# Two transformer blocks on one core: four PSUM banks for the mixers' gate projections, the last one in halves, a head rotation moved, and the retention's value product in three fp32r products

## What is computed

```python
# mixer stage, each of two layers; h is the normalised x, three branches
uv, c_q, c_kv, k_rope, z, xbc, dt_raw, gates = jnp.split(h @ w_in[l], IN_OFFSETS, axis=-1)
y_a = gmlp_mixer(uv, ...)                      # "a": spatial gating
y_b = mla_mixer(c_q, c_kv, k_rope, cos, sin, ...)   # "b": attention, 8 heads
y_c = ssd_mixer(z, xbc, dt_raw, ...)           # "c": scan over two chunks of 128 tokens
g = jax.nn.sigmoid(gates).reshape(bsz, s, N_BRANCH, D_MODEL)
merged = g[:, :, 0] * (y_a @ w_branch[l, 0]) + g[:, :, 1] * (y_b @ w_branch[l, 1]) \
       + g[:, :, 2] * (y_c @ w_branch[l, 2])
x = x + merged @ w_out[l]
# retention, each of four heads: att is the weighted score matrix, vn the values
o = jnp.einsum('bhij,bhjv->bhiv', att, vn) + ...
```

## Time and profile before

| what | value |
|---|---|
| median of 3 runs | 3313.93 us (3313.74 to 3315.62) |
| profiled execution, its own time | 3314.97 us |
| its span, first to last instruction | 3313.2 us |
| mean granted TensorE clock | 0.987 |
| PE busy | 3198.2 us, 97% |
| DVE busy | 1944.1 us, 59% |
| ACT busy | 1294.7 us, 39% |
| chain that ended last | PE 89%, DVE 5%, issue 2%, ACT 2% |

### The profile page before, as it was taken

How to read it: one execution, slowest core, us unless ns; L and a number is a source line. 1 busy time by engine, 2 the same in 40 slices (tenths; PEclk the granted TensorE clock), 3 DMA queues, 4 the chain that set the end, 5 groups by cost and what they waited for, 6 DMA issues and landing times.

```text
span 3313.2 us, 42938 instructions
## 1 busy us (share of the span) xinstructions
PE 3198.2 (97%) x17262; PEld 2727.8 (82%) x17262; DVE 1944.1 (59%) x2685; ACT 1294.7 (39%) x1785; POOL 103.3 (3%) x144
## 2 busy tenths in 40 slices
PE   8999889999998899999999999999999999999898
PEld 8988779899887799788877777778887888887797
DVE  6868568867686577674243344577334753345655
ACT  5446444444464454422223322232223222245543
POOL 1000000000000000000000000000000000022000
PEclk9999999999998999999999999999999999999999
DMA  7754347767553376553323222145333533253354
GB/s 242 243 188 166 112 139 258 248 210 235 177 171 122 127 237 224 174 179 109 114 90 101 77 89 77 64 163 168 99 111 108 188 130 105 99 134 89 98 183 153
DMA packets 334911, 496.96 MB, mean 150 GB/s; under 512 B 11042, under 2 KB 221884, under 8 KB 334716
## 3 DMA queue, kind: packets, MB, share of 16 engines
q1 hardware_dynamic: 330652, 483.46, 43.9%
q0 software_dynamic: 4064, 10.77, 1.5%
HBM read 493.09 MB, written 1.10 MB: 149 GB/s over the span
## 4 chain that ended last, share of the span: by engine, by line
PE 89%; DVE 5%; issue 2%; ACT 2%; POOL 1%; DMA 0%; DVEq 0%; POOLq 0%; ACTq 0%
PE bank L531 28%; PE bank L532 28%; PE bank L533 28%; DVE wlo L1550 1%; PE bank L953 1%; ACT whi L1090 1%; PE bank L661 1%; PE bank L544 1%; PE bank L676 0%; PE bank L938 0%; POOL small L2357 0%; POOL small L2362 0%; DVE bank L2294 0%; DVE small L2290 0%; ACT npr L1498 0%
## 5 line engine op out<-in xcount | busy, mean ns | idle before, releaser
L1550 DVE TENSOR_TENSOR wlo<-raw,whi 128x1024 fp32r<-128x1024 f32 (+1 forms) x780 | 933.9, 1211 | 995.6 <-ACT whi L1090 993.7
L1090 ACT ACTIVATE whi<-raw 128x1024 fp32r<-128x1024 f32 (+1 forms) x780 | 813.5, 1049 | 1189.8 <-PE bank L533 1186.9
L531 PE MATMUL bank<-xTh,whi 128*128 128x256 f32 (+1 forms) x3200 | 1045.5, 327 | 6.1 <-DVE xTl L1606 6.0
L533 PE MATMUL bank<-xTh,wlo 128*128 128x256 f32 (+1 forms) x3200 | 1039.4, 325 | 0.0
L532 PE MATMUL bank<-xTl,whi 128*128 128x256 f32 (+1 forms) x3200 | 1039.3, 325 | 0.0
L531 PEld LDWEIGHTS bank<-xTh,whi 128*128 128x128 f32 x3200 | 610.6, 191 | 68.7 <-issue 19.7
L533 PEld LDWEIGHTS bank<-xTh,wlo 128*128 128x128 f32 x3200 | 610.3, 191 | 49.1
L532 PEld LDWEIGHTS bank<-xTl,whi 128*128 128x128 f32 x3200 | 610.7, 191 | 48.3 <-issue 0.5
L531 PE MATMUL bank<-whi,hh 128*128 128x512 f32 x968 | 377.6, 390 | 0.0
L533 PE MATMUL bank<-whi,hl 128*128 128x512 f32 x968 | 376.7, 389 | 0.0
L532 PE MATMUL bank<-wlo,hh 128*128 128x512 f32 x968 | 376.6, 389 | 0.0
(11 more groups left out here) (337 smaller groups left out, 2318.4 us busy)
## 6 DMA issues: line engine op xcount, KB each, us to landing
raw<-in_ffn_w_in_dram SPq DMA_DIRECT2D x176, 1024.0 KB, 5.4
raw<-in_ffn_w_out_dram SPq DMA_DIRECT2D x80, 1024.0 KB, 5.0
mraw<-in_w_mod_dram SPq DMA_DIRECT2D x72, 1024.0 KB, 5.1
raw<-in_w_in_dram SPq DMA_DIRECT2D x44, 1024.0 KB, 5.1
raw<-in_ret_w_in_dram SPq DMA_DIRECT2D x24, 1024.0 KB, 5.1
raw<-in_w_branch_dram SPq DMA_DIRECT2D x12, 1024.0 KB, 5.0
raw<-in_nat_w_qkv_dram SPq DMA_DIRECT2D x12, 1024.0 KB, 5.1
raw<-in_ffn_w_out_dram SPq DMA_DIRECT2D x16, 512.0 KB, 3.6
```

The costliest lines, as they stand in the source:

```text
L531: pe.matmul(ps, lh, rh, start=start, stop=False, skip_group_check=True)
L533: return pe.matmul(ps, ll, rh, start=False, stop=stop, skip_group_check=True)
L1090: nc.scalar.activation(hi, src, ACT.Copy).then_inc(*e.inc("hi", key, part))
L1550: nc.vector.tensor_tensor(lo, src, hi.bitcast(F32), ALU.subtract).then_inc(*e.inc("lo", key, part))
```

## The change

1. **Rings.** `SHORT` becomes banks 0 to 3 and `LONG` banks 4 to 7. The gates get four banks. `bp`, `ty` of `yb` and `z`, `yd` and `yo` of chunk 1 and `wop` take `SHORT`; `ty` of `merged` takes `LONG`; the sums of chunk 1 take `VALUES` and `TURNED`, which are banks of `LONG`. The neighbourhood attention's rings keep their banks under the new names.
2. **Order of the last gate.** Gate (2,1) is loaded and projected in two halves, the first around the transposes of `yb` and `z`, the second between branch products, which are reordered to (1,0), (2,0), (1,1), (2,1); the last runs whole after the transposes of `merged`.
3. **Steps on ACT and DVE.** A head step's first half stands ahead of the weight splits of that part, its exponentials behind them; DVE asks GpSimd (POOL) for the heads' norms earlier than it reads them; tile 1's rotation moves behind the merges of branch 0.
4. **Retention.** `rv` is kept as `rvh` and `rvl`, `ra` as `rah` and `ral` (7 more DVE subtractions and 3 more ACT copies of 128x512 a head), and `retained` does 36 fp32r matmuls where it did 12 plain ones. `gbm` moves to another place in SBUF, and its two loads on POOL wait for the last head's weights.

```diff
-ALL, SCORES, TURNED, VALUES, UPPER = tuple(range(8)), (0, 1, 2, 3), (4, 5), (6, 7), (4, 5, 6, 7)
+SHORT, LONG = (0, 1, 2, 3), (4, 5, 6, 7)
+ALL, TURNED, VALUES = tuple(range(8)), (4, 5), (6, 7)
...
-        def branch(br):
-            for n in range(2):
-                s.add(("b", l, br, n), rows(w["w_branch"][l, br], 0, 4, 512 * n, 512), 4, 512)
+        def branch(br, n):
+            s.add(("b", l, br, n), rows(w["w_branch"][l, br], 0, 4, 512 * n, 512), 4, 512)
         gate(0, 0)
         gate(0, 1)
-        branch(0)
+        branch(0, 0)
+        branch(0, 1)
         gate(1, 0)
         gate(1, 1)
         gate(2, 0)
-        branch(1)
-        gate(2, 1)
-        branch(2)
+        c = GATES + 2 * D + 512
+        s.add((("g", l, 2, 1), 0), rows(m, 0, 4, c, 512), 4, 512)
+        branch(1, 0)
+        s.add((("g", l, 2, 1), 1), rows(m, 4, 4, c, 512), 4, 512)
+        branch(2, 0)
+        branch(1, 1)
+        branch(2, 1)
...
-        rv = arena("rv", [P, 4, 512], 8 * KB)
+        rvh = arena("rvh", [P, 4, 512], 8 * KB, F32R)
+        rvl = arena("rvl", [P, 4, 512], 74 * KB, F32R)
         rg = arena("rg", [P, 4, 512], 16 * KB)
         ra = arena("ra", [P, 3, 512], 24 * KB)
+        rah = arena("rah", [P, 3, 512], 82 * KB, F32R)
+        ral = arena("ral", [P, 3, 512], 24 * KB, F32R)
...
-        gbm = arena("gbm", [P, 2, D], 74 * KB)
-        rcst = arena("rcst", [P, R_END], 86 * KB)
+        gbm = arena("gbm", [P, 2, D], 30 * KB)
...
-                def gate(br, n, between=lambda part: None):
-                    ps = {t: new("gp", l, br, n, t, ring=LONG if br else ALL) for t in range(2)}
+                def gate_banks(br, n):
+                    return {t: new("gp", l, br, n, t, ring=LONG if br else ALL) for t in range(2)}
+                def gate_part(br, n, ps, part):
+                    rows_by((("g", l, br, n), part // 2), ("gp", l, br, n), ps, *xT[256], 2 * part, 8, (part % 2,))
+                def gate(br, n, step=-6):
+                    ps = gate_banks(br, n)
                     for part in range(4):
-                        rows_by((("g", l, br, n), part // 2), ("gp", l, br, n), ps, *xT[256], 2 * part, 8, (part % 2,))
-                        between(part)
-                def branch(br, n, yT):
-                    token_major([("b", l, br, n)], ("bp", l, br, n), range(2), *yT)
+                        gate_part(br, n, ps, part)
+                        attention(step + part)
+                def branch(br, n, yT, ring=SHORT):
+                    token_major([("b", l, br, n)], ("bp", l, br, n), range(2), *yT, ring=ring)
...
-                        ps = new("csb", l, c, h2)
+                        ps = new("csb", l, c, h2, ring=VALUES if c else ALL)
...
+                    ps = new("csp", l, c, ring=TURNED if c else ALL)
...
+                    ps = new("cbp", l, c, ring=TURNED if c else ALL)
...
-                    ps = new("yd", l, c)
+                    ps = new("yd", l, c, ring=SHORT if c else ALL)
...
-                gate(1, 0, lambda part: (head_turned(0) if part == 1 else attention(part - 2) if part > 1 else None))
+                gate(1, 0, -2)
...
-                ps = new("yo", l)
+                ps = new("yo", l, ring=SHORT)
...
-                gate(1, 1, lambda part: attention(2 + part))
-                gate(2, 0, lambda part: attention(6 + part))
-                turn_y(("b", l), yb, 4, 256, ("yb", l))
-                turn_y(("c", l), z, 4, 256, ("yc", l))
+                gate(1, 1, 2)
+                gate(2, 0, 6)
+                g21 = gate_banks(2, 1)
+                gate_part(2, 1, g21, 0)
+                turn_y(("b", l), yb, 4, 256, ("yb", l), SHORT)
+                gate_part(2, 1, g21, 1)
+                turn_y(("c", l), z, 4, 256, ("yc", l), SHORT)
                 pe.wait_ge(*e.at("yT", ("b", l), 1))
-                for n in range(2):
-                    branch(1, n, ytT[1])
-                gate(2, 1)
+                branch(1, 0, ytT[1])
+                gate_part(2, 1, g21, 2)
+                gate_part(2, 1, g21, 3)
                 pe.wait_ge(*e.at("yT", ("c", l), 3))
                 branch(2, 0, ytT[0])
+                branch(1, 1, ytT[1])
...
+                        ps = new("ty", ("m", l), u, ring=LONG)
...
-                b2 = {t: new("bp", l, 2, 1, t) for t in range(2)}
-                rows_by(("b", l, 2, 1), ("bp", l, 2, 1), b2, *ytT[0], 0, 4, (0,))
                 merged_turned(0)
-                rows_by(("b", l, 2, 1), ("bp", l, 2, 1), b2, *ytT[0], 2, 4, (1,))
+                branch(2, 1, ytT[0])
...
+                    wo[n] = {t: new("wop", l, n, t, ring=SHORT) for t in range(2)}
...
-                pe.wait_ge(*e.at("ra", h, 2))
-                pe.wait_ge(*e.at("rv", h, 3))
+                pe.wait_ge(*e.at("ral", h, 2))
+                pe.wait_ge(*e.at("rvl", h, 3))
                 for t in range(4):
                     ps = new("rop", h, t)
                     if t < 2:
-                        pairs = [(ra[:, 0, 256 * jt + t * P:256 * jt + (t + 1) * P], jt) for jt in range(2)]
-                        pairs += [(ra[:, 1 + jt, t * P:(t + 1) * P], 2 + jt) for jt in range(2)]
+                        pairs = [(0, 256 * jt, jt) for jt in range(2)] + [(1 + jt, 0, 2 + jt) for jt in range(2)]
                     else:
-                        pairs = [(ra[:, 1 + jt, t * P:(t + 1) * P], 2 + jt) for jt in range(2)]
-                    for i, (a, j) in enumerate(pairs):
-                        m = pe.matmul(ps[:, :], a, rv[:, j, :], start=i == 0, stop=i == len(pairs) - 1)
+                        pairs = [(1 + jt, 0, 2 + jt) for jt in range(2)]
+                    for i, (u, c, j) in enumerate(pairs):
+                        cols_of = slice(c + t * P, c + (t + 1) * P)
+                        m = mm3(ps[:, :], rah[:, u, cols_of], ral[:, u, cols_of], rvh[:, j, :], rvl[:, j, :],
+                                i == 0, i == len(pairs) - 1)
...
-                def attention(i):
-                    if i < HEADS - 1:
+                def attention(i, key, part):
+                    if -1 <= i < HEADS - 1:
                         head_turned(i + 1)
...
                         h = i - 1
                         if h >= 2:
                             act.wait_ge(*e.at("op", l, h - 2))
                         A(pT[h % 2][:, :], unit("ptp", l, h)[:, 0:384], ACT.Copy).then_inc(*e.inc("pT", l, h, frees=("ptp", l, h)))
-                    if i < HEADS:
+                    after(key, part)
+                    if 0 <= i < HEADS:
...
+                for u in range(3):
+                    act.wait_ge(*e.at("ra", h, u))
+                    A(rah[:, u, :], ra[:, u, :], ACT.Copy).then_inc(*e.inc("rah", h, u))
...
+                def heads_summed(t):
+                    dve.wait_ge(*e.at("qkq", l, t))
+                    link(V.tensor_reduce(small[:, 224:240], sq[t][:, :, :], AX, ALU.add))
+                    rstd_asked(("qk", l, t), small[:, 224:240], 16, QK)
                 def heads_scaled(t):
                     a = qk[:, t, :, :]
-                    dve.wait_ge(*e.at("qkq", l, t))
-                    link(V.tensor_reduce(small[:, 224:240], sq[t][:, :, :], AX, ALU.add))
-                    rstd(("qk", l, t), small[:, 224:240], 16, QK)
+                    dve.wait_ge(*e.at("rstd", ("qk", l, t)))
                     link(TT(a, a, heads(small[:, 240:256], 16, QK), ALU.mult))
-                def heads_rotated(t):
+                def heads_rotated(t, between=lambda: None):
...
                     link(m)
+                    between()
...
+                    if 0 <= i < HEADS:
                         h = i
...
+                    if i < HEADS + 1:
+                        after(key, part)
...
                 scan_decays(0)
-                ahead(until, (("uv", l, 1), 0))
+                after((("uv", l, 1), 0), 0)
+                heads_summed(0)
+                after((("uv", l, 1), 0), 1)
                 heads_scaled(0)
                 ahead(until, (("uv", l, 1), 1))
-                heads_rotated(0)
+                heads_rotated(0, lambda: after((("uv", l, 1), 1), 1))
                 ahead(until, (("uv", l, 0), 0))
                 gate_values()
                 ahead(until, (("uv", l, 0), 1))
-                heads_scaled(1)
+                heads_summed(1)
                 spatial_weights()
                 ahead(until, (("g", l, 0, 0), 0))
+                heads_scaled(1)
                 scan_differences(0)
                 ahead(until, (("g", l, 0, 0), 1))
                 scan_weights(0)
                 ahead(until, (("g", l, 0, 1), 0))
                 spatial_rows()
-                heads_rotated(1)
                 ahead(until, (("g", l, 0, 1), 1))
                 turned_y(("a", l), 4, 256, *ytT[1])
+                dve.wait_ge(*e.at("yd", l, 0))
+                scan_decays(1)
                 scan_rows(0)
-                scan_decays(1)
                 ahead(until, ("b", l, 0, 0))
```

(41 more changed lines are left out.)

83 lines of the change are left out of this document (45 added, 38 removed).

## The result

The changed kernel takes **3236.72 us**, median of 4 runs (3235.22 to 3237.43), against 3314.53 (3313.74 to 3315.62) of the kernel before in 4 runs: ratio 0.9764, 95% interval 0.9748 to 0.9781. That is 77.8 us faster; 67.5 were forecast. The direction came out, and so did every sign that the prediction named for the profile. The sum was 10 us short: the cost put on the rotation's new place did not come, and the waits that went were worth more than their length and the clock term together. One attribution was wrong as well, as the experiments show.

What follows compares the result with a forecast made beforehand. The prediction took the kernel as TensorE-bound, PE busy 97%. Waits 44.5, clock 19.6 and value product 8.5, less 5 for the rotation, gave 67.6 us gained: forecast 3247 us, range 3238 to 3264.

Steps and rivals of the forecast that it cites:

- every sign that the prediction named for the profile: Mixer-stage PE waits 5 us or less, none from sigmoid or issue; PEclk near 1.00; `retained` 8.2 us a head.
- The rotation in its new place: Hand-over to the heads: DVE 2.3 us late, taken as 2.5 us a layer, 5 in all; bounds 0 and 8.2 a layer.
- The clock: Mixer stages: half-clock stretches go with PE's waits, 19.6 us gained; bounds 0 and 23.
- The waits: Both mixer stages: all PE waits except 0.3 us a layer go, 44.5 us gained; bounds 22 and 44.5.
- "`ytl` comes 4.1 earlier": Mixer stages: moving the rotation behind `ytl` brings it 4.1 us earlier, removing PE's 3.1 us wait.
- "gains nothing by itself": Asking POOL earlier shortens DVE's 3.01 us wait for the norms, but gains nothing beyond the `ytl` wait already counted.
- The value product: Retention: 36 fp32r matmuls take 8.17 us a head instead of 10.30, 8.5 us gained over four heads; bounds 0 and 8.5.
- (a): Rival: DVE becomes the bound at the hand-over to the heads, one lateness costing several waits; 3256 us, chance 0.17.
- (b): Rival: mixer waits go but the clock stays 0.92; 48 us gained, 3267 us, chance 0.12.
- (c): Rival: the value split does not pay, or `retained` waits for `ral`; 8.5 us less gained, 3256 us, chance 0.05.
- (e): Rival: mixer units compete in `SHORT` and half the waits turn up there; 40.5 us gained, 3274 us, chance 0.03.
- (d): Rival: `SHORT` with four banks makes every head step wait, PE at 1.2 GHz; slower, 3340 us, chance 0.03.

Runs made afterwards that it cites:

- the rings alone: Kernel before with only the new rings (four and four banks, same users as in the change), every order as before: 3279.03 us, ratio 0.9891.
- The question alone: Kernel before with only tile 1's norms read later than asked of POOL, behind the spatial weights and splits: 3305.10 us, ratio 0.9972.
- with ACT's order: Kernel before with tile 1's norms read later than asked, and ACT rounding both weight parts of gate (0,0) ahead of the scan's exponentials: 3303.98 us.

## Why the prediction was right, and where wrong

The time fell 1.3 us below the range. On the scale of the profiles 78.3 us were gained for 67.6 of the sum; the 10.7 us between them are 4.2 for the rotation, 4.7 for what the waits cost beside their length, 1.9 outside the stages, less 0.1 in the waits.

- **The rotation in its new place** (5 us of cost): this is the step that failed. 0.7 - 0.3 = 0.4 us a layer was measured, 0.8 in all. The forecast had DVE need 27.5 us of work and 3.7 of idle time, 31.2 in all, for 28.9 of PE. Measured are 26.2 and 2.8, 29.0 in all. 1.2 of the work is a weight split that the new order of the head steps puts behind the maxima, which the sum left inside; and the idle time shrank by more than half, because it was waits for buffers and scores that come at PE's pace, so that a DVE which comes later waits less.
- **The clock** (19.6 forecast): PE's busy time fell by 24.3 at equal work, 4.7 more. Of these, 1.3 are the clock itself: 20.9 by PE's busy time at 1.2 GHz. The forecast's way to it, the loss of the mean clock times PE's busy share of 0.86 and 0.85, was sound; in the stretches PE was busy for 0.90 and 0.85 of the time. The other 3.4, most likely the edges of the waits, were in no term: the sum had a wait cost its own length and nothing at its ends.
- **The waits** (44.5 us forecast): 43.6 measured, 44.4 without the 0.8 that is counted above. Gates' banks, `ytl`, `xTl`, `yb`'s cover: all as forecast in size. That rings and order are needed together was in no term but that of `yb`: the rings alone leave or uncover some 10 us of waits a layer.
- **"`ytl` comes 4.1 earlier" by the move**, and the early question "gains nothing by itself": wrong attribution with the right total. The question alone took the wait from 3.1 to 1.5 and gained 9.9 us on the kernel before; with ACT's order 0.4 is left; the rotation's place is worth nothing on the changed kernel. That the term came out all the same is luck: the forecast gave the whole wait to one edit and nothing to the other, and the change had both.
- **The value product** (8.5): 8.6 in the kernel with it alone. The four passes of true FP32 that the Trainium skill has ("FP8 and Floating Point Precision", "TensorE Precision Notes") would have made it 10.9 by an estimate; the measurement stays with the rows.
- **Outside these stages** 1.9 us more were gained: 4.9 less of waits, 3.0 more of busy time. No term had them, and no run isolates them. The largest piece, waits for `xTl` (6.0 us in all before, 0.3 after), is 5.3 and 4.7 in two kernels that don't differ from the changed one there, so it is not put down to the change.
- **Rivals.** (a) came out only when 4.1 us of load were added, and then at 5.2 a layer, one wait and not several. (b) and (c) fell with the window rows. (e) did not come: no wait for a bank of `SHORT` is left in the changed kernel, and in the rings alone the new waits are for `yb`, `pr` and splits, not for banks. (d) fell: the window of the first head steps after, 354 to 410 us, stands at 1.00 with PE busy 55.3 of 56 us, with four banks. The rule of the Trainium skill on cycling through PSUM banks ("TensorE: Matmul & The Clock Gate", "A second HAM failure mode: psum-queue depth-cycling") does not bite here; in the mixer windows of this trace no wait of PE is for a bank.
- **The range** was too narrow at its low end: it held the rotation at no cost (3241) and 3 us for everything else, 2.4 of them for the rule on true FP32, which did not come. Nothing stood for the clock's upper bound of 23, and the busy time fell even beyond that. And all that was missing lay on the same side.
